# A two-layer diffusion step on one core: 64 instead of 32 tokens of the third block fetch their u rows, with the picks and the weight stores rearranged

## The reference, cut to what matters

```python
q = (x @ w_q).reshape(T, 8, 2, 128)                       # 8 heads, two halves
scores = jnp.einsum('thsd,hskd->thsk', q, sub_keys)       # 128 keys a half
s, i = lax.top_k(scores, 16)                              # 16 best of each half
cand = s[:, :, 0, :, None] + s[:, :, 1, None, :]          # 256 sums
top, sel = lax.top_k(cand, 16)                            # 16 best pairs
idx = i0 * 128 + i1 of the chosen pairs;  g = softmax(top)
a = gelu(einsum('td,thkd->thk', x, u_tab[idx]))           # 128 experts a token
out = einsum('thk,thkd->td', g * a, v_tab[idx])           # tables: 16384 x 1024
```

## Time and the profile before

| what | value |
|---|---|
| runs | 4046.1, 4059.3, 4049.3 us; median 4049.3 |
| the profiled execution | 4057.0 us; span from first to last instruction 4055.1 us |
| granted TensorE clock, mean | 0.978 of full speed |
| TensorE / VectorE / ScalarE / GpSimd busy | 95 / 65 / 17 / 36% of the span |
| DMA | 1155.6 MB, mean 285 GB/s |
| first expert layer | from about 555 to 2131 us; the second from about 2470 to 4022 us |

### The profile page before, as it was taken

How to read it: one execution, slowest core, us unless ns; L and a number is a source line. 1 busy time by engine, 2 the same in 40 slices (tenths; PEclk the granted TensorE clock), 3 DMA queues, 4 the chain that set the end, 5 groups by cost and what they waited for, 6 DMA issues and landing times.

```text
span 4055.1 us, 36430 instructions
## 1 busy us (share of the span) xinstructions
PE 3866.5 (95%) x12776; PEld 2211.7 (55%) x12776; DVE 2628.7 (65%) x5808; ACT 688.7 (17%) x1591; POOL 1447.8 (36%) x1180
## 2 busy tenths in 40 slices
PE   8999889999988989999998999999999899999998
PEld 1555556666656744444445545666666674444443
DVE  2682558998777955454445944998977894445444
ACT  1111011111334620000001221111143460000000
POOL 0110003554556634444320000455545663434331
PEclk9999899999989999999999999999999999999999
DMA  9452037999999999999972101899999999999994
GB/s 333 160 195 83 8 128 286 331 334 342 342 379 396 405 365 353 341 355 358 329 259 83 42 31 46 313 333 325 343 351 384 410 404 345 363 352 345 352 326 168
DMA packets 377653, 1155.57 MB, mean 285 GB/s; under 512 B 28720, under 2 KB 163360, under 8 KB 346360
## 3 DMA queue, kind: packets, MB, share of 16 engines
q0 software_dynamic: 170016, 618.96, 41.5%
q1 hardware_dynamic: 198368, 483.93, 32.7%
q10 hardware_dynamic: 9088, 50.37, 3.0%
HBM read 1055.68 MB, written 97.40 MB: 284 GB/s over the span
## 4 chain that ended last, share of the span: by engine, by line
PE 75%; DMA 10%; DVE 10%; POOL 3%; issue 1%; ACT 1%; SPq 0%; DVEq 0%; POOLq 0%
PE bank L744 74%; DMA ring<-in_peer_v,work 4%; POOL ring L696 3%; DMA ring<-in_peer_u,q_t 3%; DVE diag L1519 2%; DVE ring L1484 1%; DVE bc L1533 1%; DMA ring<-in_peer_u,work 1%; DVE bc L1531 1%; DVE ring L1651 1%; DMA bc<-peer_gates 1%; DMA ring<-in_ada_w 1%; DVE ring L1494 0%; DMA peer_gates<-work 0%; ACT hT L1050 0%
## 5 line engine op out<-in xcount | busy, mean ns | idle before, releaser
L744 PE MATMUL bank<-hT,ring 128*128 128x352 f32 (+3 forms) x5696 | 1691.8, 456 | 3.3 <-ACT hT L1050 3.3
L744 PEld LDWEIGHTS bank<-hT,ring 128*128 128x128 f32 x5696 | 1058.7, 193 | 560.7 <-issue 83.0
L696 POOL DMA_INDIRECT ring<-in_peer_u,work x512 | 753.3, 1471 | 1360.2 <-DVE ring L1484 1075.0
L744 PE MATMUL bank<-ring,work 128*128 128x512 f32 x2016 | 868.8, 592 | 0.0
L1519 DVE SCALAR_TENSOR_TENSOR diag<-ring,work,diag 128x1024 f32<-128x1024 f32 x508 | 652.5, 1285 | 96.5 <-DMA ring<-in_peer_v,work 84.4
L696 POOL DMA_INDIRECT ring<-in_peer_v,work x512 | 557.2, 1088 | 296.0 <-issue 155.2
L1484 DVE SCALAR_TENSOR_TENSOR ring<-ring,work 128x1024 f32<-128x1024 f32 x512 | 623.9, 1219 | 49.2 <-DMA ring<-in_peer_u,work 48.9
L744 PEld LDWEIGHTS bank<-ring,work 128*128 128x128 f32 x2016 | 383.0, 190 | 482.2 <-issue 482.2
L1050 ACT ACTIVATE work<-bank 128x352 f32<-128x352 f32 (+3 forms) x528 | 274.6, 522 | 1560.3 <-PE bank L744 1513.9
L744 PE MATMUL bank<-work 128*128 128x512 f32 x1056 | 461.4, 597 | 9.7 <-DVE work L1561 9.7
L1560 DVE COPY work<-bc 128x128 f32<-128x128 f32 x64 | 14.5, 227 | 663.7 <-DMA work<-peer_acts 443.7
(11 more groups left out here) (178 smaller groups left out, 2077.1 us busy)
## 6 DMA issues: line engine op xcount, KB each, us to landing
ring<-in_peer_ut SPq DMA_DIRECT2D x128, 1024.0 KB, 8.4
ring<-in_peer_vt SPq DMA_DIRECT2D x42, 2048.0 KB, 9.9
peer_gates<-work ACTq DMA_DIRECT2D x48, 1024.0 KB, 8.7
bc<-peer_gates SPq DMA_DIRECT2D x32, 1536.0 KB, 22.3
work<-in_peer_vt SPq DMA_DIRECT2D x22, 2048.0 KB, 10.3
peer_acts<-work SPq DMA_DIRECT2D x60, 704.0 KB, 6.3
work<-peer_acts SPq DMA_DIRECT2D x60, 704.0 KB, 13.9
ring<-in_ada_w SPq DMA_DIRECT2D x12, 2048.0 KB, 14.4
```

The source lines that it names most:

```text
L696: nc.gpsimd.indirect_dma_start(row, None, table, bass.IndirectOffsetOnAxis(ap=at, axis=0)).then_inc(s, 16)
L744: return nc.tensor.matmul(out, lhsT, rhs, start=start, stop=stop, **kw)
```

## The change

GQ goes from 32 to 64: 64 fetches of u rows per layer for the third block, u jobs of 320 columns, acts of 640 KB. TQ goes from 16 to 32: 12 stores of weights of 2 MB, loads in runs of 1024 bytes; the stage doubles and lies at columns 6144 to 14335 of `work`, where the first v chunk is loaded later, so that load also waits for the even stores. EARLY goes from 10 to 8.5. The first head's picks are chosen and batched in two parts, blocks 0 and 1 alone and then the others, and the sums of the exponentials (`share`) are taken out of `batch` and stand one choice later. The q loads alternate with u loads.

```diff
-TQ = 16
+TQ = 32
-GQ = 32
+GQ = 64
+TG = TQ // OH
-EARLY = 10
+EARLY = 8.5
...
-        g_stage = [work[:, 10240 + i * 2048:12288 + i * 2048].rearrange("p (j t) -> p j t", j=NKEYS) for i in range(2)]
+        g_stage = [work[:, 6144 + i * 4096:10240 + i * 4096].rearrange("p (j t) -> p j t", j=NKEYS) for i in range(2)]
...
             for c in range(CHUNKS):
-                for q in [n for n, at in enumerate((0, 0, 2, 2, 6, 6, 10, 10)) if at == c]:
-                    load_of("q", q, 2)
                 for half in range(2):
+                    for q in [n for n, at in enumerate((0, 1, 4, 5, 12, 13, 20, 21)) if at == 2 * c + half]:
+                        load_of("q", q, 2)
                     load_of("u", 2 * c + half, 2)
...
-        BATCH = (1.2, .75, .25, 1.5, 1.5, .8, .45, .3, .25, .6, .4, .1, .4)
+        BATCH = (1.2, .75, .25, 1.5, 1.5, .8, .45, .3, .25, .6, .4)
+        SHARE = (.25, .2, .4)
+        GROUPS = [(0, 0, GB), (0, GB, BLOCKS)] + [(h, 0, BLOCKS) for h in range(1, PHEADS)]
+        NG = len(GROUPS)
...
-            for h in range(PHEADS):
-                picks += [("choose", h, b, i, w) for b in range(BLOCKS) for i, w in enumerate(CHOOSE)]
-                picks += [("batch", h, 0, i, w) for i, w in enumerate(BATCH)]
+            shared = lambda s: [("share", s, 0, i, w) for i, w in enumerate(SHARE)]
+            for s, (h, b0, b1) in enumerate(GROUPS):
+                for b in range(b0, b1):
+                    picks += [("choose", h, b, i, w) for i, w in enumerate(CHOOSE)]
+                    if s and b == b0:
+                        picks += shared(s - 1)
+                picks += [("batch", s, 0, i, w * (.3 + .7 * (b1 - b0) / BLOCKS)) for i, w in enumerate(BATCH)]
+            picks += shared(NG - 1)
...
-            first = len(CHOOSE) * BLOCKS + len(BATCH)
+            first = len(CHOOSE) * GB + len(BATCH)
...
-                return ready[0][1] != "score" or q_at[2 * ready[0][2] + 1] + 2 <= n
+                return ready[0][1] != "score" or q_at[2 * ready[0][2] + 1] + (2 if ready[0][2] else 1) <= n
...
                     if n == 0:
                         sp.wait_ge(scores, (l + 1) * BLOCKS * PHEADS)
+                        sp.wait_ge(g_out[0], (l + 1) * G_OUT)
...
-                    if at == 3:
+                    if at == TG - 1:
                         act.wait_ge(sc_taken, l * len(sc_at[0]) + i + 1)
-                        nc.scalar.dma_start(gates_d[l, b * OHS // 4 + g // 4], g_stage[q % 2].rearrange("p j t -> p (j t)"))\
+                        nc.scalar.dma_start(gates_d[l, b * OHS // TG + g // TG], g_stage[q % 2].rearrange("p j t -> p (j t)"))\
                             .then_inc(g_out[q % 2], 16)
...
-                        act.wait_ge(top_ready, l * PHEADS + a + 1)
-                        f(top_e, top_e, ACT.Exp).then_inc(exp_ready, 1)
+                        _, b0, b1 = GROUPS[a]
+                        act.wait_ge(top_ready, l * NG + a + 1)
+                        f(top_e[:, b0:b1], top_e[:, b0:b1], ACT.Exp).then_inc(exp_ready, 1)
...
+                def share(s, part):
+
+                    h, b0, b1 = GROUPS[s]
...
+                    if part == 0:
+                        v.wait_ge(exp_ready, l * NG + s + 1)
+                        own.mark(v.tensor_reduce(top_s[:, b0:b1], top_e[:, b0:b1], AX.X, ALU.add))
+                    elif part == 1:
+                        own.mark(v.reciprocal(top_r[:, b0:b1], top_s[:, b0:b1]))
...
```

More of the change, by code:

```diff
@@ L241, in program @@
         onehot = bcf[:, 2048:2048 + TOPK * NP // 2].bitcast(BF16)
-        pair, side_h, which = (bcf[:, 3328 + i * 80:3408 + i * 80].bitcast(BF16).rearrange("p (k c) -> p k c", c=SIDES) for i in range(3))
+        pair, side_h, which = (bcf[:, 3328 + i * 80:3408 + i * 80].bitcast(BF16) for i in range(3))
         by16, by4, low2, mid2, off = (bcf[:, 3568 + i * 80:3648 + i * 80].bitcast(U32) for i in range(5))
@@ L280, in program @@
         top_e = small[:, 1120:1200].rearrange("p (b k) -> p b k", b=BLOCKS)
-        part_i = small[:, 1360:1520].rearrange("p (k b s) -> p b s k", b=BLOCKS, s=2)
+        part_i = small[:, 1360:1520]
         top_s = small[:, 1520:1525]
@@ L485, in peer_steps_of @@
                     ready.append((clock + 3, "gelu", a // TOPK, 0))
-                if kind == "batch" and a == PHEADS - 1 and i == len(BATCH) - 1:
+                if kind == "share" and a == NG - 1 and i == len(SHARE) - 1:
                     ready += [(clock + 1, "turn", b, 0) for b in ORDER[:-1]]
@@ L1149, in take_scatter @@
                     i = sc_at[l]["scatter", b, g]
-                    q, at = spot(b, g) // 4, g % 4
+                    q, at = spot(b, g) // TG, g % TG
                     act.wait_ge(sc_done, l * len(sc_at[0]) + i + 1)
@@ L1419, in choose, with batch @@
                         own.mark(v.max_index(top_i[:, b, 8:16], top_v[:, b, 8:16], cand_left))
-                def batch(h, part):
+                def batch(s, part):
+                    h, b0, b1 = GROUPS[s]
+                    n, lo, heads_c = b1 - b0, GB - b0, 2 * (b1 - b0)
                     at = slice(h * TOPK, (h + 1) * TOPK)
@@ L1439, in batch @@
                                                         in1=of(by16), op0=ALU.subtract, op1=ALU.max))
-                        own.mark(v.scalar_tensor_tensor(out=off, in0=top, scalar=float(WIDE * TOPK), in1=mid2, op0=ALU.is_lt, op1=ALU.mult))
-                        own.mark(v.tensor_copy(side_h.rearrange("p k c -> p (k c)"), small[:, 960:1120].bitcast(U32)))
+                        own.mark(v.scalar_tensor_tensor(out=cut(off), in0=top, scalar=float(WIDE * TOPK), in1=cut(mid2),
+                                                        op0=ALU.is_lt, op1=ALU.mult))
+                        own.mark(v.tensor_copy(in_rows(side_h), small[:, 960:1120].bitcast(U32)
+                                               .rearrange("p (k c) -> p k c", c=SIDES)[:, :, 2 * b0:2 * b1]))
                     elif part == 2:
@@ L1447, in batch @@
                     elif part == 4:
-                        own.mark(v.tensor_tensor(wide4, wide4, side_h.unsqueeze(2).to_broadcast([P, TOPK, TOPK, SIDES]), ALU.mult))
+                        own.mark(v.tensor_tensor(wide4, wide4, in_rows(side_h).unsqueeze(2).to_broadcast(wide_shape), ALU.mult))
                     elif part <= 8:
-                        n = NP * (8 >> part - 5)
-                        out = onehot[:, 0:n] if part < 8 else small[:, 1360:1520]
-                        own.mark(v.tensor_tensor(out, onehot[:, 0:n], onehot[:, n:2 * n], ALU.add))
+                        m = TOPK * heads_c * (8 >> part - 5)
@@ L1453, in batch @@
+                        out = onehot[:, 0:m] if part < 8 else part_i[:, 0:m]
+                        own.mark(v.tensor_tensor(out, onehot[:, 0:m], onehot[:, m:2 * m], ALU.add))
                     elif part == 9:
-                        own.mark(v.tensor_copy(ijg[:, :, 0:2, at], part_i[:, GB:BLOCKS, :, :]))
-                        own.mark(v.scalar_tensor_tensor(out=part_i[:, 0:GB, 0, :], in0=part_i[:, 0:GB, 0, :], scalar=float(NKEYS),
-                                                        in1=part_i[:, 0:GB, 1, :], op0=ALU.mult, op1=ALU.add))
@@ L1457, in batch @@
[L1457 to L1470, removed]
-                    else:
[L1472 to L1477, removed]
@@ new lines, in batch @@
+                        if b0 == 0:
+                            own.mark(v.scalar_tensor_tensor(out=off[:, 0:GB * TOPK].rearrange("p (b k) -> p b k", b=GB), in0=found[:, 0:GB, 0, :],
+                                                            scalar=float(NKEYS), in1=found[:, 0:GB, 1, :], op0=ALU.mult, op1=ALU.add))
+                        if b1 == BLOCKS:
+                            own.mark(v.tensor_copy(ijg[:, :, 0:2, at], found[:, lo:n, :, :]))
+                            own.mark(v.scalar_tensor_tensor(out=idx_f, in0=found[:, lo, 0, :], scalar=float(NKEYS), in1=found[:, lo, 1, :],
+                                                            op0=ALU.mult, op1=ALU.add))
+                    else:
+                        if b0 == 0:
+                            v.tensor_scalar(idx_all[:, rows_at], off[:, 0:GB * TOPK], float(l * EXPERTS), None, ALU.add).then_inc(idx_ready, 1)
+                        if b1 == BLOCKS:
+                            ins = v.tensor_scalar(idx_t[:, at], idx_f, float(l * EXPERTS), None, ALU.add)
+                            if h == PHEADS - 1:
+                                ins.then_inc(idx_t_ready, 1)
+                            else:
+                                own.mark(ins)
@@ L1578, in peer @@
                 v.wait_ge(h_ready[2 * l + 1], BLOCKS)
-                own.mark(v.tensor_copy(which, iota[:, 0:TOPK].unsqueeze(2).to_broadcast([P, TOPK, SIDES])))
+                own.mark(v.tensor_copy(which.rearrange("p (k c) -> p k c", c=SIDES), iota[:, 0:TOPK].unsqueeze(2).to_broadcast([P, TOPK, SIDES])))
                 for kind, a, b, i, _ in dve_order():
```

(2 more changed lines are left out.)

40 lines of the change are left out of this document (30 added, 10 removed).

## The result

The changed kernel takes 4121.9 us (four runs, 4111.6 to 4122.8) against 4047.7 us of the kernel before beside it: a ratio of 1.017, 95% interval 1.0154 to 1.0186. The sign was forecast, the size was not: 28 us were expected, 74 came, and the time lies 2 us above the range. The profiled execution's span is 4121.0 us for 4055.1.

What follows compares the result with a forecast made beforehand. TensorE's order bounds choosing and values, transfers the middle, transfers and VectorE the tail. Per layer -35 - 3 + 71 - 20 + 1 + 0 = +14, +28 for both on 4049.3: 4077 us, range 4010 to 4120.

Steps and rivals of the forecast that it cites:

- The turn: TensorE's turning of the picks, ending the choosing stretch: 35 us earlier per layer, at about 1028 us.
- the first groups: First 8 one-hot groups of the hot stretch: one slot less, -3 us per layer.
- the tail: Last 56 one-hot groups: fewer slots against extra one-hots, -20 us per layer (bounds -15 and -27), near 129 us.
- the values: Values stretch after the seam: pure TensorE, 661 us without gaps, change 0 per layer (bounds 0 and +26).
- VectorE's saved waits: Choosing stretch: VectorE loses 43 us of slots and most of the exponential wait, saving nothing because TensorE's order paces it.
- the exponential wait: Choosing stretch: VectorE's 32.6 us wait for exponentials behind job copies in ScalarE's order, forecast to nearly vanish.
- the middle: The 32 groups carrying u-row products: 109 MB at 391 GB/s, 278 us, +71 per layer (bounds +54 and +110).
- The ring rival: Middle: four u rows per 12.7 us bind, middle +110, +53 us per layer, 4155 us; chance 0.08.
- the seam: Store then load of weights between last one-hot and values: store +2.6, load -1.5, net +1 us (bounds -3 and +6).
- the faster one: Rival: middle at the tail's 417 GB/s, 261 us, tail at VectorE's floor, -12 us per layer, 4025 us; chance 0.30.
- The transfer-bound values stretch: Rival: a chunk's 8.05 MB needs 21.6 us against 20.7, 26 us over 28 chunks, 4129 us; chance 0.10.
- The 372: Values stretch: 372 GB/s, taken as the most this stretch shows, used to price the transfer-bound rival's chunk at 21.6 us.

Runs made afterwards that it cites:

- tq16: The changed kernel with 16 tokens per weight store instead of 32, 64 fetched tokens and all else kept: 4106.9 us, ratio 1.0141.
- b_e78_u5v3: The kernel before with EARLY at 7.8 for 10, five u rows and three v rows instead of four each: 4008.5 us, ratio 0.9881.

## Why the prediction was right or wrong

Right was what decides the sign: less work for TensorE is given back where rows are fetched. In the two expert layers TensorE is busy 51 us less, not 105, at a granted clock of 0.961 and 0.966 for 0.985 and 0.986, and idles 200 us for 84. The turn came at 1025 us (1028 forecast), the first groups at -2 (-3), the tail at 125 us (129), the values at 661 us without a gap. That VectorE's saved waits would gain nothing because TensorE's order paces the choosing was right: the turn came as early as TensorE's order had it, and new waits for scores stand in VectorE's order (15 us). That the exponential wait would nearly vanish was not (23 of 33 us stayed).

**The step that failed** is the price of the middle, 109 MB "At the rate of this same stretch, 391 GB/s, 278 us", so +71. The bytes were right (112 MB), the rate was not: 372 GB/s, 301 us, +94. I took the rate "because the same mix of transfers ran in it". It did not: u rows per group rose from two to three, and only u rows pass through the four buffers that the loop of GpSimd, transfer and VectorE was already turning over, in 12.7 us a turn. The ring rival named the mechanism, but was put at 0.08 and at a fixed 12.7 us a turn, 317 us. The measured turn is 11.9 us. With five buffers the middle took 278 us: the byte price holds once the ring does not bind, though its bytes and its rate (111 MB, 400 GB/s) are each 2% above the forecast's and cancel. That this kernel's 4077.7 us meet the forecast of 4077 is in part luck: in its trace the two expert layers are 12 and 11 us longer than before, where 14 each were forecast. Between the two profiled executions lie 66 us for the 28 forecast. The middle's part of that gap is 23 us in the first layer and 17 in the second, where it took 295 us for 207; the seam's is 3 and 4, and choosing and tail gave a few microseconds back.

The second mis-sized term is the seam: +1 forecast, +4 measured, with the store 3.8 us longer (2.6 forecast) and the load 1.2 us longer (1.5 shorter forecast). The doubled runs do not show as a gain on the path, and tq16 gets the whole seam back.

Of the other rivals: the faster one needed the middle above 413 GB/s, and no kernel with 64 tokens ran it above about 400. The transfer-bound values stretch did not come: 379 GB/s in this kernel and 385 in b_e78_u5v3, at most 4 us of gaps. The 372 that I took for the most this stretch can have came from one row of 50 us. Its share of 1.01 looks full, yet with the same runs of 512 B the stretch held 377 in tq16 and 385 in b_e78_u5v3 for 620 us, so that row showed no ceiling. The limit of about 358 GB/s of HBM for one core (the Trainium skill, "DMA: Bandwidth & Descriptors", section Specifications, where it is half of a stack's 716) is passed in the values stretch of the changed kernel by 21 GB/s for 620 us; the measurement decides. The 372 passed it already, so the old values stretch did not agree with it either.

What the prediction did not see at all is that the loss was not in the arrangement as a whole: EARLY at 8.5 by itself gains 40 us. The groups then end while TensorE still has jobs that cover the seam; that is 9 us of it, and the rest are fewer waits for one-hots and a clock that falls less, whose cause was not tried apart. The 64 tokens take jobs away and lengthen the groups: the changed kernel has 5 jobs left in its tail for 17 before, waits there for one-hots, and has the seam open again.

Open: what a faster issue or another order of use would win on the turn was not tried. When each u fetch of the changed kernel's middle is matched with its product and with the next fetch into its buffer, the mean turn is 12.3 us: 1.2 of issue, 8.9 until the product starts, 1.2 of product and 0.9 until GpSimd issues again. Landing is most of it. Nor was it tried which of split, sums, load order and stores costs the 23 us at EARLY 10; TensorE idles 20 us more there than in the kernel before, 14 of them at the seam that the larger stores lengthen.

## What to carry to other kernels

Price a stretch that fetches through a ring twice, by bytes at a rate and by buffers per turn, and take the longer; a rate read from a stretch holds for its ratio of ring rows to other bytes. Work taken off the busiest engine is lost where it covered another engine's work or a serial seam: first look which engine ends the stage last. A rate read from one short stretch is no ceiling, even at a share of 1.0.

## What the runs showed of the hardware that was not expected

With three, four and five u rows in flight (and five, four and three v rows), one buffer's turn takes 9.9, 11.9 and 14.0 us, while the fetches land in 7.0 to 8.2, 8.8 to 9.0 and 9.9 us; the transfers' share is 0.90, 0.97 and 1.00, at 333, 372 and 400 GB/s. The values stretch ran at 377 GB/s with runs of 512 B without a gap for TensorE.

A full share is not one rate, since it counts the time of packets. In the values stretch of the kernel before, a packet of 512 B held its DMA engine for 30 ns on average, one of 4096 B for 179 and one of 16 KB for 650; after, one of 1024 B took 48 ns. That is 17, 23, 25 and 21 GB/s for an engine.

In the tail, where 5 of TensorE's jobs are left for 17 before and it is busy 96 of 125 us for 138 of 149, its granted clock is 0.83 on average (0.98 before), so some of its time there is at the lower level, 1.2 GHz for 2.4.
